# Mixer of an mLSTM and Hyena block: first steps' inputs loaded in the hyena tail, keys and values asked for apart, an earlier modulation turn

## Reference

```python
shift, scale, gate = split(silu(c) @ w_mod + b_mod)              # the same for the context, from c_ctx
h = rms_norm(x, pre_gain) * (1 + scale) + shift
qk, v, o, zm, g, hy, zh = split_proj(h @ w_in)
# (A) mLSTM, 4 heads x 128, both directions, chunk by chunk (state C, n, stabiliser m):
s   = (q_c @ k_c.T) * exp(dmat - m_t)                             # inside a chunk
num = s @ v_c + exp(inter - m_t) * (q_c @ C)                      # and from the state
C   = exp(b_last + m - m_new) * C + (exp(src - m_new) * k_c).T @ v_c
m_l = rms_norm(h_f + h_b gated by sigmoid(o)) * mh_gain * silu(zm)
# (B) Hyena: two gated long convolutions of 512 channels, by FFT, gated by silu(zh)
y   = concatenate([m_l, y_hy]) @ w_out
out = x + gate * rms_norm(y, post_gain)
```

## Time and profile before

| | |
|---|---|
| median of 3 runs | 1599.39 us (1598.91 to 1602.81) |
| the profiled execution | 1599.17 us, its span 1597.4 us |
| TensorE busy | 1532.2 us, 96% of the span |
| VectorE, ScalarE, POOL busy | 43%, 40%, 20% |
| DMA | 201.92 MB, 40% of 16 engines |
| projection | first product at 43.73 us |
| chunks of the mixer | from about 1271.8 us |
| steps of the mixer | from about 1322.6 us to the end |

### The profile page before, as it was taken

The page is one execution under the profiler, slowest core; times in us unless marked ns, Lnnn a source line. Parts: engine busy times, 40 slices in busy tenths (PEclk is TensorE's granted clock), DMA queues, the critical chain, the costliest instruction groups (busy, mean ns, idle before and its releaser), DMA issues. The chain is left out here.

```text
span 1597.4 us, 22990 instructions
## 1 busy us (share of the span) xinstructions
PE 1532.2 (96%) x8892; PEld 1344.4 (84%) x8892; DVE 691.2 (43%) x1129; ACT 633.5 (40%) x1357; POOL 311.7 (20%) x298
## 2 busy tenths in 40 slices
PE   4899999999999999999999999999999887999997
PEld 2788888888888888888888899999999776888886
DVE  1654430233333333000020377777765477555553
ACT  2785312343222222122111355445454385555551
POOL 1652000000000000000000031211213136666661
PEclk8899999999999999999999999999999899999999
DMA  8342621222222222112122464656446494666651
GB/s 345 102 125 71 234 74 56 77 73 73 79 72 74 77 72 80 71 46 99 53 77 73 169 172 123 185 136 181 111 106 157 173 270 139 199 196 196 201 185 53
DMA packets 128276, 201.92 MB, mean 126 GB/s; under 512 B 12571, under 2 KB 75793, under 8 KB 121270
## 3 DMA queue, kind: packets, MB, share of 16 engines
q1 hardware_dynamic: 128182, 200.64, 40.0%
HBM read 122.57 MB, written 52.86 MB: 110 GB/s over the span
## 5 line engine op out<-in xcount | busy, mean ns | idle before, releaser
L514 PE MATMUL bank<-h_hi,w_hi 128*128 128x512 f32 (+1 forms) x800 | 310.9, 389 | 11.7 <-DVE w_lo L848 9.7
L516 PE MATMUL bank<-h_hi,w_lo 128*128 128x512 f32 (+1 forms) x800 | 309.0, 386 | 0.0
L515 PE MATMUL bank<-h_lo,w_hi 128*128 128x512 f32 (+1 forms) x800 | 308.9, 386 | 0.0
L514 PEld LDWEIGHTS bank<-h_hi,w_hi 128*128 128x128 f32 x800 | 151.4, 189 | 42.1 <-ACT w_hi L654 9.8
L516 PEld LDWEIGHTS bank<-h_hi,w_lo 128*128 128x128 f32 x800 | 151.4, 189 | 30.1
L515 PEld LDWEIGHTS bank<-h_lo,w_hi 128*128 128x128 f32 x800 | 151.5, 189 | 29.6 <-issue 0.2
L912 DVE SCALAR_TENSOR_TENSOR work<-work,coef 128x504 f32<-128x504 f32 (+1 forms) x84 | 63.2, 753 | 237.2 <-ACT work L674 237.1
L514 PE MATMUL bank<-w_hi,h_hi 128*128 128x512 f32 (+1 forms) x448 | 164.5, 367 | 0.0
L515 PE MATMUL bank<-w_lo,h_hi 128*128 128x512 f32 (+1 forms) x448 | 164.1, 366 | 0.0
L516 PE MATMUL bank<-w_hi,h_lo 128*128 128x512 f32 (+1 forms) x448 | 164.1, 366 | 0.0
L664 ACT ACTIVATE work<-bank 128x512 f32<-128x512 f32 (+1 forms) x72 | 40.4, 562 | 296.8 <-PE bank L516 296.8
(11 more groups left out here) (249 smaller groups left out, 2801.7 us busy)
## 6 DMA issues: line engine op xcount, KB each, us to landing
H<-spectrum SPq DMA_DIRECT2D x192, 128.0 KB, 2.3
stage<-in_w_in SPq DMA_DIRECT2D x18, 1024.0 KB, 5.6
s_hy<-work SPq DMA_DIRECT2D x48, 256.0 KB, 2.2
x<-s_hy SPq DMA_DIRECT2D x8, 1024.0 KB, 5.0
kq<-s_k SPq DMA_DIRECT2D x32, 256.0 KB, 4.5
v<-s_v SPq DMA_DIRECT2D x32, 256.0 KB, 5.2
mb<-s_rows SPq DMA_DIRECT2D x32, 256.0 KB, 5.6
late<-in_x SPq DMA_DIRECT2D x16, 512.0 KB, 4.8
```

Source lines behind the costliest of these rows:

```text
L514: pe.matmul(out, lhs[0], rhs[0], start=(k == 0), stop=False)
L515: pe.matmul(out, lhs[0], rhs[1], start=False, stop=False)
L516: return pe.matmul(out, lhs[1], rhs[0], start=False, stop=(k == KD - 1))
```

## The change

Six edits. (1) `turn_mod(2)` is done after piece c = 6 instead of after the loop. (2) Keys and values of a chunk have a semaphore each (`k_in`, `v_in`): the turn waits for keys alone, the increments for values. Keys of chunk c are asked for after the turn of chunk c - 4 (`k_turned`), values as before after its increments; the first queries of the steps are asked for by `k_turned` too. (3) Rows `mb` of step 0, `og` and `zg` of steps 0 and 1, and `gate` are loaded by `early.load` in the hyena tail instead of between the chunks; they, `gains` and `power` get places in that memory, and one semaphore `steps_in` counts the mask, `mpb` and all of these. (4) `HIGH_WO` becomes a map from chunk to piece: the hyena half is rounded in chunks 2 to 5, pieces 1, 2, 3, 0 of the mLSTM half in 6 to 9. (5) `backward(0, NT_LAT)` moves into VectorE's iteration 13 of the chunks. (6) In a step the rows `mb` are asked for before `k`, `q` and `v`, and in step 1 ScalarE does `high_mlstm(0)` before `weights(2, 1)`.

```diff
-                if c in (2, 4):
+                if c in (2, 4, 6):
                     turn_mod(c // 2 - 1)
-            turn_mod(2)
             turn_mod(3)
...
-HIGH_WO = (2, 3, 4, 5, 6, 7, 8, 9)
+HIGH_WO = {2: 4, 3: 5, 4: 6, 5: 7, 6: 1, 7: 2, 8: 3, 9: 0}
+WO_NTH = {k: i + 1 for i, k in enumerate(HIGH_WO.values())}
+STEPS_IN = 160
+BACKWARD_AT = 13
...
-    def load_kv(self, sp, s, c):
+    def load_k(self, sp, s, c):
         slot = c % SLOTS
-        sp.dma_start(self.kq[:, slot], s["k"][c]).then_inc(self.kv_in[slot], 16)
+        sp.dma_start(self.kq[:, slot], s["k"][c]).then_inc(self.k_in[slot], 16)
+
+    def load_v(self, sp, s, c):
+        slot = c % SLOTS
         sp.dma_start(self.v1[:, slot, :, 0:DH], s["v"][c].rearrange("p (h v) -> p h v", h=HEADS))\
-          .then_inc(self.kv_in[slot], 16)
+          .then_inc(self.v_in[slot], 16)
...
+        for dr in range(2):
+            sp.dma_start(self.mb[:, 0, dr], rows_of(s, dr, LAST)).then_inc(self.steps_in, 16)
+        for b in range(2):
+            sp.dma_start(self.og[:, b].rearrange("p h v -> p (h v)"), s["ozh"][0, LAST - b]).then_inc(self.steps_in, 16)
+            sp.dma_start(self.zg[:, b].rearrange("p h v -> p (h v)"), s["ozh"][1, LAST - b]).then_inc(self.steps_in, 16)
+        sp.dma_start(self.gate[:, :], spread(s["gate"][0])).then_inc(self.steps_in, 16)
...
-            def load_kv(c):
+            def load_k(c):
+                sp.wait_ge(k_turned, c - SLOTS + 1)
+                early.load_k(sp, s, c)
+
+            def load_v(c):
                 sp.wait_ge(uf_ready, c - SLOTS + 1)
                 sp.wait_ge(ub_ready, backward_done(c - SLOTS))
-                early.load_kv(sp, s, c)
+                early.load_v(sp, s, c)
...
-                c = NT - 3 - n
-                sp.wait_ge(uf_ready, c + 1)
-                sp.wait_ge(ub_ready, backward_done(c))
+                sp.wait_ge(k_turned, NT - 2 - n)
                 sp.dma_start(qT[:, kv_slot(n)], s["q"][lat(n)]).then_inc(step_in[n % 2], 16)
...
                 sp.wait_ge(num_ready, n - 1)
+                load_rows(n)
                 sp.dma_start(kT[:, slot], s["k"][t + NT_CTX]).then_inc(step_in[b], 16)
                 sp.dma_start(qT[:, slot], s["q"][t]).then_inc(step_in[b], 16)
                 sp.dma_start(v1[:, slot, :, 0:DH], s["v"][t + NT_CTX].rearrange("p (h v) -> p h v", h=HEADS))\
                   .then_inc(step_in[b], 16)
-                load_rows(n)
...
+            load_k(SLOTS)
             for c in range(SLOTS, NT):
-                load_kv(c)
-                if c == 5:
+                if c + 1 < NT:
+                    load_k(c + 1)
+                load_v(c)
+                if c == 7:
                     sp.wait_ge(early.y_out, 16 * GROUPS)
                     load_yh(0)
-                    load_rows(0)
-                if c == 7:
+                if c == 9:
                     load_rows(1)
-                if c == 9:
-                    load_fin(0)
-                if c == 11:
-                    sp.dma_start(gate[:, :], spread(s["gate"][0])).then_inc(gate_in, 16)
                 if c == 13:
                     load_yh(1)
-                if c == 15:
-                    load_fin(1)
...
-                pe.wait_ge(kv_in[c % SLOTS], 32 * (c // SLOTS) + 32)
+                pe.wait_ge(k_in[c % SLOTS], 16 * (c // SLOTS) + 16)
...
             def increments(c):
+                pe.wait_ge(v_in[c % SLOTS], 16 * (c // SLOTS) + 16)
...
+                if n == 1:
+                    high_mlstm(0)
                 if n + 1 < NT_LAT:
                     weights(n + 1, 1)
-                if 0 < n <= NT_LAT:
+                if 1 < n <= NT_LAT:
                     high_mlstm(n - 1)
...
-            backward(0, NT_LAT)
+            for c in range(NT):
+                if c != 2:
+                    weigh_backward(c)
+                if c:
+                    forward(c - 1)
+                if HIGH_WO.get(c - 1, KD) < HEADS:
+                    low_wo(HIGH_WO[c - 1])
+                if c == BACKWARD_AT:
+                    backward(0, NT_LAT)
```

More of the change, by code:

```diff
@@ L1105, in __init__ @@
         self.gain = at("gain", [P, HEADS], 20352)
+        self.gains = at("gains", [P, HEADS], 20448)
+        self.power = at("power_m", [P, 2, HEADS], 20384)
+        self.power_o = at("power_o", [P, 2], 20416)
         self.raw_offset = base + X_AT
         self.raw = at("wo_raw", [P, KD, D], X_AT)
-        self.kv_in = [sem(f"kv_in{i}") for i in range(SLOTS)]
-        self.wc_in = sem("wc_in")
-        self.mpb_in = sem("mpb_in")
+        self.og = at("og", [P, 2, HEADS, P], X_AT + 32768)
+        self.zg = at("zg", [P, 2, HEADS, P], X_AT + 36864)
+        self.gate = at("gate", [P, D], X_AT + 40960)
+        self.mb = at("mb", [P, 2, 2, HEADS, P], X_AT + 45056)
+        self.k_in = [sem(f"k_in{i}") for i in range(SLOTS)]
+        self.v_in = [sem(f"v_in{i}") for i in range(SLOTS)]
+        self.steps_in = sem("first_steps_in")
         self.cols_in = sem("cols_in")
@@ L1150, in mixer @@
         sb("raw_m", [P, KD * D])
[L1151 to L1154, removed]
+        sb("steps_m", [P, 3 * D])
+        sb("mb_m", [P, 2 * D])
         den = sb("den", [P, 2, HEADS])
@@ L1175, in mixer @@
         raw, mask, gain = early.raw, early.mask, early.gain
+        og, zg, gate, mb = early.og, early.zg, early.gate, early.mb
+        gains, power, power_o = early.gains, early.power, early.power_o
         cols, mpb, wc = early.cols, early.mpb, early.wc
@@ L1197, in mixer @@
         wo_low_h = sem("wo_low_h")
-        kv_in = early.kv_in
+        k_in, v_in = early.k_in, early.v_in
         k_turned = sem("k_turned")
@@ L1360, in _ @@
             pool.wait_ge(const_set, 5)
-            pool.wait_ge(early.mpb_in, 48)
+            pool.wait_ge(early.steps_in, STEPS_IN)
             def cover(n):
@@ L1551, in _ @@
         def _(act):
-            act.wait_ge(early.cols_in, 16)
+            act.wait_ge(early.cols_in, 48)
             def weigh_forward(c):
@@ L1670, in _ @@
         def _(dve):
-            dve.wait_ge(early.cols_in, 16)
+            dve.wait_ge(early.cols_in, 48)
             def weigh_backward(c):
@@ L1696, in low_wo @@
             def low_wo(k):
-                dve.wait_ge(wo_high, k + 1)
+                dve.wait_ge(wo_high, WO_NTH[k])
                 dve.scalar_tensor_tensor(w_lo[:, k, :], raw[:, k, :], gains[:, k:k + 1],
                                          w_hi[:, k, :].bitcast(F32), ALU.mult, ALU.subtract).then_inc(wo_low_m, 1)
-            dve.wait_ge(early.wc_in, 32)
-            for c in range(NT):
-                if c != 2:
-                    weigh_backward(c)
-                if c:
-                    forward(c - 1)
-                if c - 1 in HIGH_WO[:HEADS]:
-                    low_wo(HIGH_WO.index(c - 1))
             def backward(c, slot):
```

48 lines of the change are left out of this document (22 added, 26 removed).

## The result

The changed kernel takes 1604.54 us (median of 18 runs, 1599.02 to 1607.35) beside 1598.73 us for the kernel before on the same chips (18 runs, 1593.12 to 1603.35). The ratio is 1.0030, with an interval of 1.0019 to 1.0041: slower, where 1592.8 us, faster, was forecast. The profiled execution took 1601.35 us. It lies only 2.2 us above the profiled one of the kernel before, where the medians lie 5.8 us apart; what the other executions lost beyond that no trace shows.

What follows compares the result with a forecast made beforehand. TensorE, busy almost all of the span, was taken as the bound. Start 1.0, chunks and state 3.3, steps 0.8 and clock 1.5 made 6.6 us off 1599.17, plus 0.2 for the median: 1592.8 us; range 1588.5 to 1597.0.

Steps and rivals of the forecast that it cites:

- Later steps: Mixer from 1372 to 1579 us: TensorE busy 205.43 of 207 us, so earlier inputs were worth nothing.
- The rows asked for first: Mixer's first steps, POOL's wait at cover(3): an earlier last landing was to give between nothing and 1.16 us.
- the wait for all five loads stays: Rival, mixer steps: rows first does nothing, the rest holds; 4.3 us, 1595.1 us; inside the forecast's range, no separate chance.
- Start of the projection: Modulation turns before the projection: turn_mod(2) fits TensorE's idle time before c = 7; gain 1.0 us.
- Chunks 2.2 us: The mixer's 18 chunks: DMA waits vanish, ScalarE weighs chunk 14 earlier; gain 2.2 us, bounds 0.5 and 4.0.
- state 1.1 us: Step 0: moving backward(0) to iteration 13 lets products start earlier; gain 1.1 us, bounds 0.5 and 1.3.
- The moved transfers: Hyena tail: seven more DMAs, 2 MB, about 7 us at 300 GB/s, were to cost nothing.
- `high_mlstm(0)`, 0.5 us: Step 1: high_mlstm(0) ahead of weights(2, 1) starts the first output product 0.5 us earlier.
- The 0.3 us for the stall behind `cover(3)`: Early steps: part of the 0.8 us step term, for a shorter TensorE stall at 1356.83 us.
- third rival: Mixer steps: the shared wait for five loads stays, rows first does nothing; 4.3 us, 1595.1 us; no separate chance.
- VectorE and POOL collide: Rival, chunks: their low parts block each other, up to 10.3 us lost, 1603.1 us; chance 0.04.
- 1.5 of 4.8 us: Half clock stretches at the projection's start (2.0 us) and behind the 1356.83 stall (2.8 us): 1.5 us counted.

Runs made afterwards that it cites:

- a_rows_last: Changed kernel with the stabiliser rows of a step asked for behind keys, queries and values again; 1.0000 of the kernel before.
- b_turn: Kernel before with one edit, the third modulation turn placed after piece c = 6; 1.0008 of the kernel before.
- before_again: Kernel before, unchanged, profiled a second time; one execution, 1598.37 us.
- a_place_rows_own: Changed kernel, rows on their own semaphore from step 2 on, 96 bytes ahead of wo_hi restoring the old addresses; 1591.51 us, 0.9939 of the kernel before.
- a_place_rows_last: Changed kernel, rows asked for behind keys, queries and values, 96 bytes ahead of wo_hi restoring the old addresses; 0.9965 of the kernel before.

## Why the prediction was wrong, point by point

**Later steps "bound by matmuls, and an edit that makes their inputs earlier is worth nothing there".** This is the step that failed. That no gain was to be had was right; I took it to mean that no loss was to be had either, and the sum has no term for one. TensorE was the bound, but only just. The chain behind it runs: rows asked for, last transfer landed, `cover`, ScalarE's `weights(n+1, 0)`, its squares of the step before, VectorE's gate and sum, SP's store, the next x, the next rows. In the changed kernel, SP's issues and POOL's `cover` between them:

```profile
1404.70 1.52 SPq L1306 DMA_DIRECT2D mb<-s_rows  x2
...
1420.36 0.34 SPq L1343 DMA_DIRECT2D out<-late  x1
...
1421.27 1.46 SPq L1306 DMA_DIRECT2D mb<-s_rows  x2
```
```profile
1414.04 2.51 POOL L1390 TENSOR_TENSOR late<-mb,mask 128x512 f32<-128x512 f32 x2 [1.99 <-DMA v<-s_v]
```

From issue to `cover` 9.34 us, from there to the next issue 7.23: 16.57 us, more than the 16.15 that TensorE needs. The same in `a_rows_last`, where keys are asked for first:

```profile
1402.45 0.79 SPq L1316 DMA_DIRECT2D kq<-s_k  x1
...
1418.48 0.79 SPq L1316 DMA_DIRECT2D kq<-s_k  x1
```
```profile
1411.30 2.52 POOL L1390 TENSOR_TENSOR late<-mb,mask 128x512 f32<-128x512 f32 x2 [1.85 <-DMA mb<-s_rows]
```

8.85 and 7.18: 16.03, under 16.15. The second part is never under 7.16 us in any trace; in the changed kernel it is 7.17 to 7.23 in each of ten steps, with no time to spare. In the kernel before, the mean from issue to `cover` was 8.7 us: 15.9 with the 7.2, beside TensorE's 15.84. There was no room for a later landing. Of the 7.7 us lost in the twelve steps 4.2 are waits that this loop made; the other 3.7 are the pace, below, less the 0.2 us that the kernel before waited too. The loop explains why the changed kernel gained nothing from a better place (1.0030, 1.0037, 1.0021 at 92000, 92032, 92096) while the one with its own count did (1.0001, 0.9978, 0.9939).

**The rows asked for first help "by what the last landing is earlier when it is a value load: between nothing and 1.16 us".** I had the sign wrong, and the bound from one side only. From issue to landing, values in the changed kernel and in `a_rows_last` (lowest, median, highest):

```profile
DMA to landing us min/median/max: 5.4/6.6/7.7
```
```profile
DMA to landing us min/median/max: 4.2/5.2/5.9
```

The rows' two transfers landed a median of 5.7 us behind their issue when asked for first and 5.5 when last, but values behind them in the queue take 1.4 us more. The last landing of five moves back: first issue to `cover` has a mean of 9.55 us against 8.7 before. Already `cover(3)` shows it, in the changed kernel:

```profile
1347.09 2.49 POOL L1390 TENSOR_TENSOR late<-mb,mask 128x512 f32<-128x512 f32 x2 [2.04 <-DMA v<-s_v]
```

2.04 us of waiting where it was 1.16, and the stall behind it grew from 3.23 to 4.09 us. The rival "the wait for all five loads stays" named this wait, priced it as nothing gained, and went no further. Its price, across batches: 4.6 us where the weights stand as in the changed kernel (1.0030 against 1.0001), 13 us at 92096 (1.0021 against 0.9939), and 7.0 us alone on the kernel before.

**The place of the weights: foreseen nowhere.** `gains`, `power` and `power_o`, 32 bytes each in the built program, left the place ahead of the weights, so that what lies behind them moved by 96 bytes. 0.31 us a step is 4.6 us over 15 steps. The shorter period is shown; in medians the move from 92032 to 92096 gave 0.4% (0.9978 to 0.9939, in different batches), or 6 us, somewhat more than 15 times 0.26.

**Start of the projection, 1.0 us: nothing.** The prediction had the case ("at half clock it would end at 28.9 and take back 0.35 us") and was still too mild. In the changed kernel the clock fell right behind the matmuls of c = 6, so the turn took 1.82 us, c = 7 had to wait for it, and its row's copy, which the turn used to cover, left TensorE idle for 0.70 us. In `b_turn`: 1.87 us less behind c = 7, but 1.87 - 0.56 = 1.31 more ahead of it (TensorE had idled 0.56 there in `before_again`) and 0.70 of waiting for the copy, together 0.14 us later. Over all traces the first product starts at a mean of 44.1 us with the turn moved (12 traces, 42.3 to 45.1) and 43.5 without (8 traces, 42.4 to 44.7): nothing, or a small loss. The Trainium skill ("TensorE: Matmul & The Clock Gate", Part 1, "What's actually happening") holds that the clock is low by default and that activity lifts it, and the prediction read this as speaking for the turn. The turn did not bear that reading out: it ran at or near half clock (1.69 to 1.87 us) in ten of the twelve traces.

**Chunks 2.2 us and state 1.1 us: right, and larger.** 3.63 to the scores and 0.90 more to the products of step 0, 4.53 against 3.3, inside the bounds. TensorE's waits for DMA are gone between 1271.5 and 1322; its longest wait there, 1.68 us ahead of the increments at 1311.58, ended with ScalarE's weighing at 1311.48 and came back within 0.01 us in two other kernels of this family. ScalarE weighed chunk 14 at 1305.54, 3.5 us earlier counted from the first turn, where 2.2 was worked out. VectorE and ScalarE in the changed kernel:

```profile
1291.20 1.28 DVE L1716 SCALAR_TENSOR_TENSOR wo_lo<-wo_raw,gains,wo_hi 128x1024 fp32r<-128x1024 f32 x1
...
1299.70 1.28 DVE L1716 SCALAR_TENSOR_TENSOR wo_lo<-wo_raw,gains,wo_hi 128x1024 fp32r<-128x1024 f32 x1
...
1306.14 1.14 DVE L1727 SCALAR_TENSOR_TENSOR CB<-CB,wc 128x129 f32<-128x129 f32 x4
```
```profile
1305.54 1.15 ACT L1577 ACTIVATE kw<-psS,cols 128x128 f32<-128x128 f32 x4
```

The four low parts are 2.83 us apart, as worked out, but ran from 1291.20, where I had put the first at 1293.5: VectorE was through 2.3 us sooner, 0.9 of it because the chunks began that much earlier. For the state moved, the recorded 1.1 us should have been 1.0 by its own rows (1324.58 less 1323.6).

**The moved transfers, nothing: right.** In the changed kernel the last of them is issued at 1256.60 us and the store of the last y at 1270.10 (1271.01 before), so the store isn't late.

**`high_mlstm(0)`, 0.5 us: right.** 0.60 more at the output product (2.09 us of waiting to 1.55). The 0.3 us for the stall behind `cover(3)` became a loss of 1.0. (The third rival's 4.3 us leaves this 0.5 out, though it stays with the order of the loads; it should have been 4.8 or so.)

**VectorE and POOL collide: not there, but the price is real.** POOL's four low parts ran from 1278.88 for 9.49 us and were through at 1288.4, ahead of VectorE's first. That this rival's 1603.1 us lies near the measured 1604.54 is chance. The mechanism shows up where `cover` starts early. VectorE's update of `CB` in the steps of `a_place_rows_own` and of `a_place_rows_last`, 1372 to 1550 (busy, mean ns):

```profile
L1735 DVE SCALAR_TENSOR_TENSOR CB<-CB,wc 128x129 f32<-128x129 f32 x44 | 36.1, 878 | 0.0
```
```profile
L1728 DVE SCALAR_TENSOR_TENSOR CB<-CB,wc 128x129 f32<-128x129 f32 x44 | 12.5, 345 | 0.0
```

In one step of the former, POOL's `cover` and VectorE's four operations:

```profile
1408.14 2.60 POOL L1399 TENSOR_TENSOR late<-mb,mask 128x512 f32<-128x512 f32 x2
```
```profile
1408.10 3.32 DVE L1735 SCALAR_TENSOR_TENSOR CB<-CB,wc 128x129 f32<-128x129 f32 x4
```

3.32 us for what takes 1.13 alone, while POOL loses at most 0.1: VectorE is the one held. It costs nothing here: every period of that kernel is 15.84 us. The Trainium skill ("SBUF — State Buffer", "Who interferes with whom") holds that a VectorE operation with two inputs in SBUF and a GpSimd operation that reads SBUF contend, and that one is blocked while the other runs. By it VectorE would be held for up to POOL's 2.60 us, an estimate; the trace, with 2.2, agrees roughly.

**Clock.** The forecast took 1.5 of 4.8 us. The half clock stretch behind the stall at 1356.83 was there in the changed kernel too, only shorter (1351 to 1357 us: 0.72, then 1.00): from the end of the stall to the scores of step 3 it took 7.22 us instead of 8.47, so the clock did give back about 1.25 us. In the three kernels with a count of their own the stall is 2.03 us, and the clock stays at 1.00 behind it. Window 1357 to 1369 of the kernel before, then of `a_place_rows_own`:

```profile
1357.00:1369.00 12.00, 12.00 (x45) 0.75 0.63 197
```
```profile
1357.00:1369.00 12.00, 12.00 (x77) 1.00 0.61 200
```

But `a_place_rows_last` had 1.00 there behind a stall of 2.81 us as well; no rule can be drawn from these. In span, the fastest version stands 7.8 us below the kernel before: 4.5 up to the scores of step 1, 4.6 from there to those of step 3 (1.2 is the shorter stall, 3.0 the clock: 12 us at 0.75), 0.2 behind, less 1.5 by which its chunks began later. Its median is 9.8 us lower by the ratio; those 2 us more are not explained.

## What to carry to other kernels

"The bound engine is busy all the time" rules out gains, not losses: before an edit to the loads of such a stage, add up the loop that returns to the load's issue, through the queue that issues it, and compare it with the bound engine's period; in the kernel before they were 15.9 and 15.84 us. When several transfers share one count, the order in which they are asked for doesn't matter to the consumer, only the last landing does; to serve one early, give it a count of its own. When tiles are added or moved, keep the old addresses of operands that a long run of matmuls streams, or measure the run's pace: 96 bytes cost 2% of a step here.

## What the runs showed of the hardware

- The start address of `wo_hi` and `wo_lo`, the moving operands, set the pace of these 128x512 fp32r matmuls, 0.227 to 0.234 us from start to start at full clock, reproducibly in every step; 92096 and 92352 are equally good (0.227 to 0.229), 92000 is the worst (0.234), 92032 and 92128 are next (0.233). Matmuls that stream other tiles kept their pace.
- The values of a step, issued as the last of five transfers or as the third, land a median of 6.6 or 5.2 us behind their issue; the two transfers of rows land at 5.7 us, issued first, and 5.5, issued last. Which transfers stand ahead matters by 1.4 us.
- Two operations of VectorE and POOL that both work from SBUF: VectorE's four took 3.32 us instead of 1.13 beside POOL's 2.60, and POOL lost at most 0.1.
